# Long convolutions at half-shifted frequencies, filters made between the projection slabs, and expert rows fetched on ScalarE's queue

## What is computed

```python
u = up[:, :-2] * conv_w[0] + up[:, 1:-1] * conv_w[1] + up[:, 2:] * conv_w[2] + conv_b
x1, x2, v = jnp.split(u, 3, axis=-1)          # 512 channels each
z = v
for n in range(2):
    zf = jnp.fft.rfft(z, n=2 * S, axis=1)
    conv = jnp.fft.irfft(zf * kf[None, :, n], n=2 * S, axis=1)[:, :S]
    z = gates[n] * (conv + skip[n] * z)       # gates = (x1, x2)
```

## Time and profile before

| | us |
|---|---|
| median of 3 runs | 4476.01 |
| lowest, highest | 4473.81, 4476.74 |
| profiled execution, its own time | 4471.62 |
| its span in the trace | 4469.8 |
| PE busy | 3871.2 (87%) |
| DVE busy | 1572.0 (35%) |
| ACT busy | 850.8 (19%) |
| POOL busy | 817.9 (18%) |
| share of PE in the chain that ended last | 68% |

### The profile page before, as it was taken

How to read it: one execution, slowest core, us unless ns; L and a number is a source line. 1 busy time by engine, 2 the same in 40 slices (tenths; PEclk the granted TensorE clock), 3 DMA queues, 4 the chain that set the end, 5 groups by cost and what they waited for, 6 DMA issues and landing times.

```text
span 4469.8 us, 81395 instructions
## 1 busy us (share of the span) xinstructions
PE 3871.2 (87%) x35878; PEld 2676.6 (60%) x35878; DVE 1572.0 (35%) x2802; ACT 850.8 (19%) x1380; POOL 817.9 (18%) x568
## 2 busy tenths in 40 slices
PE   7896888986886788997999996995999999987997
PEld 3362335552332356764888883544888888855775
DVE  1262221121111565543343344022555544423233
ACT  1132001111110213421111111112222332202221
POOL 0000000001112000001232210004445444403441
PEclk9996999988988899999999998997999999988999
DMA  3124004416787010002111111331000000011221
GB/s 132 66 109 161 10 10 151 160 67 240 294 332 272 24 38 10 1 29 85 63 61 66 57 66 57 123 142 65 3 22 13 13 13 13 3 49 57 86 103 48
DMA packets 63822, 370.28 MB, mean 83 GB/s; under 512 B 12800, under 2 KB 12800, under 8 KB 26224
## 3 DMA queue, kind: packets, MB, share of 16 engines
q1 hardware_dynamic: 43488, 304.11, 17.9%
q0 software_dynamic: 19840, 59.90, 3.6%
q10 hardware_dynamic: 144, 1.05, 0.1%
HBM read 375.49 MB, written 39.85 MB: 93 GB/s over the span
## 4 chain that ended last, share of the span: by engine, by line
PE 68%; DVE 8%; PEld 6%; DMA 5%; issue 4%; POOL 3%; ACT 3%; SPq 0%; PEldq 0%; DVEq 0%; ACTq 0%; POOLq 0%
PE psum L448 31%; PE psum L460 5%; PE psum L461 4%; PE psum L462 4%; PE psum L628 3%; DMA arena<-moe_rows 3%; PE psum L1715 2%; PE psum L2273 2%; PE psum L2260 2%; PE psum L503 2%; PEld psum L460 2%; PEld psum L461 2%; PE psum L647 2%; PEld psum L462 2%; PE psum L546 2%
## 5 line engine op out<-in xcount | busy, mean ns | idle before, releaser
L448 PE MATMUL psum<-arena 64*64 64x64 f32 (+4 forms) x14328 | 784.9, 246 | 75.4 <-POOL arena L2496 22.7
L448 PE MATMUL psum<-arena,ring 128*128 128x512 f32 (+2 forms) x2176 | 802.2, 527 | 22.9 <-DVEq L3397 8.9
L448 PEld LDWEIGHTS psum<-arena 64*64 64x64 f32 (+3 forms) x14328 | 580.3, 143 | 248.8 <-issue 185.8
L448 PEld LDWEIGHTS psum<-arena,ring 128*128 128x128 f32 (+1 forms) x2176 | 408.8, 189 | 415.4 <-issue 380.4
L476 POOL TENSOR_TENSOR ring_low<-ring,slab_high 128x2048 fp32r<-128x2048 f32 x66 | 303.7, 4615 | 1336.0 <-ACT slab_high L469 1335.9
L460 PE MATMUL psum<-h_high,slab_high 128*128 128x512 f32 (+1 forms) x1056 | 380.4, 360 | 42.0 <-DVE h_low L491 30.5
L461 PE MATMUL psum<-h_low,slab_high 128*128 128x512 f32 (+1 forms) x1056 | 377.4, 357 | 0.0
L462 PE MATMUL psum<-h_high,ring_low 128*128 128x512 f32 (+1 forms) x1056 | 377.1, 357 | 0.0
L460 PEld LDWEIGHTS psum<-h_high,slab_high 128*128 128x128 f32 x1056 | 202.1, 191 | 79.8 <-issue 36.2
L462 PEld LDWEIGHTS psum<-h_high,ring_low 128*128 128x128 f32 x1056 | 202.1, 191 | 28.5
L461 PEld LDWEIGHTS psum<-h_low,slab_high 128*128 128x128 f32 x1056 | 202.4, 192 | 27.6
(11 more groups left out here) (313 smaller groups left out, 4674.1 us busy)
## 6 DMA issues: line engine op xcount, KB each, us to landing
ring<-in_wall SPq DMA_DIRECT2D x181, 1024.0 KB, 6.1
arena<-in_wall SPq DMA_DIRECT2D x96, 1024.0 KB, 11.2
moe_rows<-arena POOLq DMA_DIRECT2D x2, 6144.0 KB, 31.6
arena<-moe_rows SPq DMA_DIRECT2D x24, 512.0 KB, 9.8
moe_out<-arena POOLq DMA_DIRECT2D x24, 512.0 KB, 8.6
arena<-spill POOLq DMA_DIRECT2D x8, 1024.0 KB, 5.6
spill<-arena POOLq DMA_DIRECT2D x2, 3072.0 KB, 16.9
arena<-in_tabs POOLq DMA_DIRECT2D x1, 2624.0 KB, 10.2
```

What stands on the lines that cost most here:

```text
L448: last = L.eng.matmul(out, a, b, start=(i == 0), stop=(i == len(pairs) - 1))
```

## The change

The frequencies are shifted by half a step, so that there is no zero and no Nyquist frequency, and tokens are split into even and odd ones. Frequencies f and 511-f then share the products over the tokens of one parity, and differ only in a sign between even and odd. 256 frequencies are computed, the others follow by sums and differences. Slab order, filters, products and the expert rows change as follows.

```diff
-    plain(..., ("in_krs", 1), ("in_hy", 6), ("uq", 1), ..., ("mod", CONV_MODS),
-          ("decay", 1), ("hw3", 1), ("skip0", 1), ("out", 4), ...
+    plain(..., ("in_krs", 1), ("decay", 1), ("hw3", 1), ("in_hy", 6), ("uq", 1), ..., ("mod", CONV_MODS),
+          ("skip0", 1), ("out", 4), ...
 def mix_in_tensor(L, m, B):
     project_tensor(L, m, "in_q", h, [(0, T)], ready=1)
+    sine_tensor(L, m, m.vec("hw1", 0, 64, parts=33), B.zemb)
...
+    sine_tensor(L, m, m.vec("hw2", 0, 64, parts=64), B.h1)
...
-    project_tensor(L, m, "in_hy", h, [(0, T)])
+    filter_tensor(L, m, B)
+    for i in range(6):
...
+        if i < 2:
+            L.eng.wait_ge(m.sem("filter_parts"), L.nth("filter_parts"))
...
+            spectrum_tensor(L, B.early, lambda t: B.sums[:, t, :], lambda t: B.filt[i][:, t, 0:HW])
+def spectrum_tensor(L, tabs, even_part, odd_part):
+    for g in range(2):
+        f = slice(g * P, (g + 1) * P)
+        for part, even, odd in ((even_part, tabs.even_c, tabs.odd_c), (odd_part, tabs.even_s, tabs.odd_s)):
+            for first, table in ((0, even), (2, odd)):
...
+                matmuls(L, ps, [(table[:, k, f], part(first + k)) for k in range(2)]).then_inc(L.bank_full, 1)
+def filter_spectrum_vector(L, m, B, order):
...
+            L.eng.scalar_tensor_tensor(low, ps, 2.0 / L2, e, ALU.mult, ALU.add)
+            if part == 0:
+                L.eng.scalar_tensor_tensor(high, ps, -2.0 / L2, e, ALU.mult, ALU.add).then_inc(L.bank_free, 1)
...
+def inverse0_tensor(L, m, B):
+    for g in range(2):
+        L.eng.wait_ge(m.sem("products"), L.nth("products"))
+        for t in range(4):
...
+            pairs = [(B.dft.inv_c, sr), (B.dft.inv_s, si)] if t < 2 else [(B.dft.odd_c, dr), (B.dft.odd_s, di)]
+            for i, (table, y) in enumerate(pairs):
+                last = L.eng.matmul(ps, table[:, g, s], y, start=(g == i == 0), stop=(g == i == 1))
+def long_tensor(L, m, B):
+    L.eng.wait_ge(m.sem("convolved"), L.nth("convolved", 4))
+    turned = turn_tensor(L, m, lambda d, i: B.hu[:, 8 + i, tokens(d)])
+    L.eng.wait_ge(m.sem("dft_landed"), L.nth("dft_landed", 16))
...
+    spectrum_tensor(L, B.dft, lambda t: B.vt[:, t, :], lambda t: B.vt[:, t, :])
...
+    turn_tensor(L, m, lambda d, i: B.hu[:, i, tokens(d)])
+    inverse0_tensor(L, m, B)
...
+    L.eng.wait_ge(m.sem("gated"), L.nth("gated", 4))
+    spectrum_tensor(L, B.dft, lambda t: B.vt[:, t, :], lambda t: B.vt[:, t, :])
+    turn_tensor(L, m, lambda c, t: B.vt[:, t, c * P:(c + 1) * P])
+    inverse1_tensor(L, m, B)
+def product_vector(L, m, B, order):
+    first = halves_vector(L, m, B, 0)
+    second = halves_vector(L, m, B, 1)
+    L.eng.wait_ge(*first)
+    low_vector(L, m, B, 0, order)
+    join_vector(L, m, B, 0)
+    L.eng.wait_ge(*second)
+    low_vector(L, m, B, 1, order)
+    join_vector(L, m, B, 1)
+def long_pool(L, m, B):
...
+    for order in range(2):
+        for g in range(2):
...
+            L.eng.wait_ge(m.sem("high_half"), L.nth("high_half"))
+            e.tensor_tensor(yr, zr, kr, ALU.mult)
...
+            e.tensor_tensor(yi, yi, zi, ALU.add).then_inc(m.sem("high_product"), 1)
         def _(pool):
-            load(m.xc[:, :, :], a["ctx"], "inputs_landed")
+            load(B.zemb, ..., "dft_landed")
+            load(B.early.all, tab("dft", 3072), "dft_landed")
             load(m.at(28184, 1024), tab("cos96", 1024), "rope96")
+            load(m.xc[:, :, :], a["ctx"], "ctx_landed")
+            for order in range(2):
...
+                pool.dma_start(m.filters[order], B.kout[order]...).then_inc(m.sem("filter_stored"), 16)
             L.eng.wait_ge(m.sem("room_for_dft"), L.nth("room_for_dft"))
-            load(B.dft, tab("dft_c", 5248), "dft_landed")
+            load(B.dft.all, tab("dft", 3072), "dft_landed")
+            for order in range(2):
+                load(B.kf[order]..., m.filters[order], "filter_landed")
...
+            long_pool(L, m, B)
 def moe_sync(sp, m, B, wall):
-        sp.dma_start(B.hg[i % 2], m.moe_rows[pair_rows(i), :]).then_inc(m.sem(f"pair_rows{i % 2}"), 16)
+def pair_rows_scalar(L, m, B, i):
+    if i >= 2:
+        L.eng.wait_ge(m.sem("pair_turned_low"), i - 1)
+        L.eng.wait_ge(m.sem("pair_turned_high"), i - 1)
+    L.eng.dma_start(B.hg[i % 2], m.moe_rows[pair_rows(i), :]).then_inc(m.sem(f"pair_rows{i % 2}"), 16)
 def moe_scalar(L, m, B):
         if i + 1 < NPAIR:
             pair_turn_scalar(L, m, B, i + 1)
+            pair_rows_scalar(L, m, B, i + 3)
```

More of the change, by code:

```diff
@@ L1106, in turn_tensor, with turn_scalar, sine_tensor @@
         last.then_inc(L.bank_full, 1)
[L1109 to L1120, removed]
+        turned.append(L.read_out)
+    return turned
+def turn_scalar(L, m, dst):
+    for d in range(4):
+        ps = L.next_bank()
+        L.eng.wait_ge(L.bank_full, L.fill)
+        out, src = dst(d, ps)
+        L.eng.activation(out, src, ACT.Copy).then_inc(L.bank_free, 1)
+    L.eng.wait_ge(*L.read_out)
+def sine_tensor(L, m, w, x):
+    if "dft_landed" not in L.counts:
+        L.eng.wait_ge(m.sem("dft_landed"), L.nth("dft_landed", 32))
     ps = L.next_bank()
@@ new lines, in inverse1_tensor @@
+def inverse1_tensor(L, m, B):
+    L.even_bank()
+    banks = []
+    for g in range(2):
+        L.eng.wait_ge(m.sem("products"), L.nth("products"))
+        sr, dr, si, di = [B.y[:, 4 * g + i, :] for i in range(4)]
+        for c in range(4):
+            s = slice(c * P, (c + 1) * P)
+            if g == 0:
+                banks.append((L.next_bank(2), L.bank_full))
+                for bank_free, count in L.bank_frees:
+                    L.eng.wait_ge(bank_free, count)
+            ps, full = banks[c]
+            for p, pairs in enumerate((((B.dft.inv_c, sr), (B.dft.inv_s, si)), ((B.dft.odd_c, dr), (B.dft.odd_s, di)))):
+                for i, (table, y) in enumerate(pairs):
+                    last = L.eng.matmul(ps[:, BANK * p:BANK * p + T // 2], y[:, s], table[:, g, :], start=(g == i == 0), stop=(g == i == 1))
+            if g == 1:
+                last.then_inc(full, 1)
@@ L1312, in inverse1_vector, with halves_vector @@
-def inverse1_vector(L, m, B):
-    for c in range(4):
-        t1 = B.tmp[:, 0, :]
+        L.eng.activation(B.even[:, i, :], ps, ACT.Copy).then_inc(L.bank_free, 1)
+        L.next_bank()
+def halves_vector(L, m, B, g):
+    e = L.eng
+    for part in range(2):
+        L.next_bank()
+        copied, even = L.read_out, B.even[:, 2 * g + part, :]
+        ps = L.next_bank()
+        L.eng.wait_ge(*copied)
+        L.eng.wait_ge(L.bank_full, L.fill)
+        low, high = B.y[:, 4 * g + part, :], B.y[:, 4 * g + 2 + part, :]
+        if part == 0:
+            e.tensor_tensor(high, even, ps, ALU.subtract)
+        else:
+            e.tensor_tensor(high, ps, even, ALU.subtract).then_inc(m.sem("high_half"), 1)
+            L.nth("high_half")
+        e.tensor_tensor(low, even, ps, ALU.add).then_inc(L.bank_free, 1)
+    return L.read_out
@@ new lines, in join_vector @@
+def join_vector(L, m, B, g):
+    e = L.eng
+    yr, yi, hr, hi = B.low[:, 0, :], B.low[:, 1, :], B.high[:, 2 * g, :], B.high[:, 2 * g + 1, :]
+    sr, dr, si, di = [B.y[:, 4 * g + i, :] for i in range(4)]
+    L.eng.wait_ge(m.sem("high_product"), L.nth("high_product"))
+    e.tensor_tensor(sr, yr, hr, ALU.add)
+    e.tensor_tensor(dr, yr, hr, ALU.subtract)
+    e.tensor_tensor(si, yi, hi, ALU.subtract)
+    e.tensor_tensor(di, yi, hi, ALU.add).then_inc(m.sem("products"), 1)
+    L.eng.wait_ge(m.sem("products"), L.nth("products"))
```

524 lines of the change are left out of this document (262 added, 262 removed).

## The result

The changed kernel takes 4281.1 us (median of 4 runs, 4272.3 to 4290.0) against 4474.9 for the kernel before in the same rounds: a ratio of 0.9565, 95% interval 0.9542 to 0.9587. The forecast was 4268, the range 4228 to 4318: sign and range were right, the time came out 13 us above the forecast. Between the two profiled executions it is 4471.62 - 4285.34 = 186.3 us, where the sum said 208. The 21.7 us that are missing there can be placed by stage.

The account below looks back on a forecast made before the run. PE's matmuls and holes were taken to bound the convolutions, PE's waits for rows to slow the experts. Start -5, projections +48, convolutions -203, experts -48: -208 from 4471.6, 4263.6; plus 4.4 for the median, 4268. Range 4228 to 4318.

Parts of the forecast that it names:

- Start and projections: Up to the first modulation matmul: start -5 us, work added to the projections +48, together +43.
- slow restart after it, 2.9: Projections: after the 65-row filter matmuls PE restarts at reduced clock, costing 2.9 us.
- The rival with +14: Projections: the 65-row filter matmuls run at half clock, +14 us; chance 0.10, shared with late filter loads.
- At an even share the last modulation slab comes later by some 2.2 us: Modulation: with POOL's loads sharing full DMA engines, the last slab comes some 2.2 us later.
- my own bound of 6: Modulation: upper bound on the last slab's delay by POOL's loads, 6 us; the lower bound was 0.
- The long chain: Long convolutions: hand-laid chain from the turn of v at 336.5 to 426.1, where before it was 629; -203 us.
- low product 6 x 0.73 = 4.4, join 4 x 0.69 = 2.9: Long convolutions: DVE's low product and join after a spectrum, 4.4 and 2.9 us, part of 8.8 in order 1.
- Experts: Experts' stage: rows asked for earlier on ACT's queue; seven waits remain of fourteen, for weights; -48 us.
- The lower bound, -101 with no wait left: Experts: no wait is left, -101 us instead of -48, total 4215; chance 0.07.
- The rule that spoke against the experts' part: Experts: skill page says spreading transfers over issuing engines brings no bandwidth; by it the term would be 0.
- Signs of being wrong: Prediction wrong if PE waits for loads in the convolutions, or the experts' stage is not between 330 and 365 us.
- third rival: Long convolutions: POOL's second high product and DVE's low product and join exclude each other; +15, 4283; chance 0.20.

Follow-up runs that it names:

- filters_late: The kernel after with zeros issued early and the two filter loads held until the ninth modulation slab: 4275.2 us, ratio 0.9559.
- pool_first_group: The kernel after with POOL's high-frequency product of the second group given to DVE, POOL keeping the first group's: 4270.4 us, ratio 0.9544.
- gates_first: The kernel after with gate and up slabs of both regular pairs of a group asked for before either's down slabs: 4273.0 us, ratio 0.9528.
- no_overflow: The kernel after with both regular pairs' gate and up slabs first and the overflow pairs' indirect weight fetch left out: 4236.3 us, ratio 0.9479.
- rows_sp_ahead: The kernel after with expert rows back on SP's queue, asked for one pair ahead, before the previous pair's weights: 4281.7 us, ratio 0.9549.

## Why the prediction was right, and where its sum was off

- **Start and projections**: +41.3 for +43. The count of matmuls held (13.98, 14.00 and 13.97 us a block). The term "slow restart after it, 2.9" was wrong: the clock was full before, in and after the filter block. The rival with +14 did not come either: matmuls of 65 rows that began at full clock kept it. In the kernel before they began at half clock, behind holes, and did not regain it in 27.67 us, where 128 rows did within 6. The 128 rows had an even longer slow stretch in front of them, so the number of rows is the likelier reason, but no run takes it apart.
- **"At an even share the last modulation slab comes later by some 2.2 us"**: mis-sized, 9.4 measured, above my own bound of 6. Of it 8.35 us are the three waits. The even share was worked out for one slab. The last of the loads, 5.5 MB in all, lands 26 us after its issue, and over that time three slabs fell behind, each making PE wait. `filters_late` gave 8.2 us of it back. An estimate by bytes would have come nearer: the filters' 4.2 MB at the 423 GB/s of the earlier trace rows are 10 us of full DMA engines.
- **The long chain**: 89.6 forecast from the turn to the last gated result, 99.3 measured to the norm. Piece by piece: turn 4.5 for 4.1, first spectrum 16.2 for 16.8, **product and join 14.3 for 8.8**, inverse 17.9 for 18.6, second spectrum 14.0 for 13.9, **product and join 14.2 for 8.8**, last inverse 18.1 for 18.6. Only DVE's part was off, by 10.9 us in sum. The step that failed is "low product 6 x 0.73 = 4.4, join 4 x 0.69 = 2.9": those durations are of a DVE without POOL beside it. I had priced the rest as a rival (+15, chance 0.20) and left it out of the likeliest sum. The first price, 7.6 us in each order, supposed that POOL's whole product goes first. In fact the two take turns, one operation each: from 406.90 to 417.93 seven DVE operations ran beside six of POOL's and took 11.0 us. The same seven without POOL took 4.7 us (419.85 to 424.56). So DVE lost 6.3 us an order, and the rest of its chain was 0.8 shorter than priced, which leaves the 5.4 to 5.5. `pool_first_group` confirms it: 7.9 us less although DVE does more.
- **Experts**: -44.8 for -48, by the mechanism forecast: seven places of fourteen remain, at the second regular pair of each group, waiting for weights. They cost 7.7 us each on average for the 7.5 forecast, which is 1.2 of the 3.2 us; the other 2.0 are not placed. `gates_first` confirms the reason (its gate slabs stood behind down slabs that waited for an output). The lower bound, -101 with no wait left, missed that the overflow pair's fetch is next in line. `no_overflow`, with the gate slabs first and without that fetch, takes 301.0 us, 91 less than before: the DMA engines would nearly do it otherwise.
- **The rule that spoke against the experts' part** spoke of bytes, as I read it. `rows_sp_ahead` shows it.
- **Rest of the kernel**: +5.5 that no part of the change makes.
- **Signs of being wrong**: neither came. From 385 to 484 us PE waits for no load, and the experts' stage is 347.5 us. The waits for loads stood just in front, in the modulation, where the prediction had named no sign.
- **Likeliest case and what came**: the measured 4281.1 is nearer to the third rival's 4283 than to the forecast. That rival's mechanism did come, with 10.9 us of its 15. But that the total meets its number is partly chance, as the slabs, the experts and the rest of the kernel made up for what it lacked.

In sum: 7.2 for the slabs, 9.7 for the chain, 3.2 for the experts, 5.5 for the rest, less 1.7 for the projections, 1.6 for the stage between and 0.7 of rounding (629 for 629.68): 21.6 of the 21.7.

## What to carry to other kernels

When work moves from one engine to two, price the slower copy of each instruction: look for a stretch of the old trace in which both engines read two SBUF operands, and if there is none, put their contention into the sum and its absence among the rivals. Where a transfer waits behind others, ask what is asked for first, not on which queue; and when that wait goes, name the next one in the same order (rows, then gate slabs, then the indirect fetch). A large load issued early is not free where the DMA engines are already full: here the 4 MB of filters cost 8 us of modulation, and of the 8 us that holding them back gave, 6 were lost again because they then landed late.

## What the runs showed of the hardware that was not expected

- DVE and POOL slow each other, but do not shut each other out for whole instructions. A DVE operation of 0.69 us and a POOL operation of 1.27 have 1.96 us in sum; side by side a pair takes 1.69 on average (six POOL starts from 407.41 to 415.87). Which part of an instruction is shut out, the rows don't tell. The Trainium skill, page "SBUF — State Buffer", section "Who interferes with whom", says that a DVE instruction with two SBUF inputs contends with a GpSimd instruction that reads SBUF. The runs agree on that, and they show one PSUM operand free of it (0.68 us beside POOL's 1.27 to 1.29).
- The indirect fetch of rows that are mostly skipped costs 31 us of stage time though it moves few bytes (POOL's queue moved 15.5 MB with it and 16.8 without from 886 to 1236 us): with the same slab order the rate is 416 to 427 GB/s without it, and with it there is a slice of 256 to 291 in each of six groups, where the DMA engines had too little to do.
- Sixteen matmuls of 65 rows ran at full granted clock (1.00), 13.98 us, behind a busy PE at full clock. Begun at half clock behind holes, they stayed at 0.50 for all of their 27.67 us.
